# A relative-position bias that is shifted through DRAM, written and read back in four pieces

## What is computed

```python
delta = qi + BLOCK - kj
bucket = t5_causal_bucket(np.clip(delta, 0, steps) * dilation)
bias = jnp.transpose(rel_bias_table.astype(jnp.float32)[bucket], (2, 0, 1))
scores = jnp.einsum('brhnqd,brhnkd->brhnqk', qb, kw).astype(jnp.float32) * (dh ** -0.5)
scores = jnp.where(valid, scores + bias[None, None, :, None], NEG_INF)
```

```python
h = rmsnorm(x, g[0])
z = h @ w_in
za, zb, zc = jnp.split(z, [3 * A_WIDTH, 3 * A_WIDTH + 2 * B_WIDTH], axis=-1)
```

## Time and profile before

| | |
|---|---|
| median of 3 runs | 2355.29 us (2349.98 to 2355.97) |
| the profiled execution | 2355.84 us, span 2354.1 us |
| TensorE matmul busy | 2253.3 us, 96% of the span |
| VectorE, ScalarE, GpSimd busy | 1362.3, 1067.9, 62.9 us |
| mean granted clock of TensorE | 0.979 of full speed |
| moved by DMA | 375.59 MB, 160 GB/s over the span |

### The profile page before, as it was taken

How to read it: one execution, slowest core, us unless ns; L and a number is a source line. 1 busy time by engine, 2 the same in 40 slices (tenths; PEclk the granted TensorE clock), 3 DMA queues, 4 the chain that set the end, 5 groups by cost and what they waited for, 6 DMA issues and landing times.

```text
span 2354.1 us, 31707 instructions
## 1 busy us (share of the span) xinstructions
PE 2253.3 (96%) x12978; PEld 1959.9 (83%) x12978; DVE 1362.3 (58%) x1718; ACT 1067.9 (45%) x1376; POOL 62.9 (3%) x66
## 2 busy tenths in 40 slices
PE   8799999888989999999999999999999999999998
PEld 7788898787877888888888888888986889889776
DVE  5446666566556666767666444655445555544554
ACT  5343542424455544544555334545435443544443
POOL 0000101002000000000000000000000000000000
PEclk9899999899989999999999999999999999999999
DMA  7756440014634555555565555553550556445143
GB/s 279 189 191 202 163 158 1 1 32 154 203 118 134 190 185 188 186 187 187 186 206 191 190 192 196 185 195 120 181 178 19 180 178 222 159 152 174 59 129 140
DMA packets 237804, 375.59 MB, mean 160 GB/s; under 512 B 8535, under 2 KB 110072, under 8 KB 236920
## 3 DMA queue, kind: packets, MB, share of 16 engines
q1 hardware_dynamic: 229596, 362.83, 46.3%
q10 hardware_dynamic: 8092, 11.11, 1.9%
HBM read 369.45 MB, written 4.46 MB: 159 GB/s over the span
## 4 chain that ended last, share of the span: by engine, by line
PE 65%; issue 5%; DVE 4%; ACT 2%; POOL 0%; DVEq 0%; POOLq 0%; ACTq 0%
PE PS L482 16%; PE PS L441 12%; PE PS L443 12%; PE PS L442 12%; PE PS L485 8%; DVE w_lo L359 1%; PE PS L2062 1%; ACT w_hi L354 1%; PE PS L2152 1%; PE PS L2136 1%; PE PS L2046 1%; PE PS L2827 1%; DVE h_both L938 0%; PE PS L921 0%; ACT spare L2074 0%
## 5 line engine op out<-in xcount | busy, mean ns | idle before, releaser
L359 DVE TENSOR_TENSOR w_lo<-raw,w_hi 128x2048 fp32r<-128x2048 f32 (+2 forms) x340 | 766.8, 2256 | 765.2 <-ACT w_hi L354 765.0
L354 ACT ACTIVATE w_hi<-raw 128x2048 fp32r<-128x2048 f32 (+2 forms) x340 | 641.2, 1886 | 876.0 <-PE PS L443 494.4
L482 PE MATMUL PS<-h_both,w_hi 128*128 128x512 f32 x1968 | 541.6, 397 | 12.2 <-DVE w_lo L359 9.4
L441 PE MATMUL PS<-w_hi,h_both 128*128 128x512 f32 (+2 forms) x1344 | 514.9, 383 | 11.7 <-DVE h_both L943 4.5
L442 PE MATMUL PS<-w_lo,h_both 128*128 128x512 f32 (+2 forms) x1344 | 507.2, 377 | 0.0
L443 PE MATMUL PS<-w_hi,h_both 128*128 128x512 f32 (+2 forms) x1088 | 408.3, 375 | 0.0
L482 PEld LDWEIGHTS PS<-h_both,w_hi 128*128 128x128 f32 x1968 | 338.1, 190 | 59.4 <-ACT arena L609 9.6
L485 PEld LDWEIGHTS PS<-h_both,w_lo 128*128 128x128 f32 x1968 | 303.2, 189 | 42.2
L485 PE MATMUL PS<-h_both,w_lo 128*128 128x256 f32 x1968 | 314.0, 281 | 0.0
L441 PEld LDWEIGHTS PS<-w_hi,h_both 128*128 128x128 f32 x1344 | 254.3, 189 | 60.0 <-issue 6.0
L442 PEld LDWEIGHTS PS<-w_lo,h_both 128*128 128x128 f32 x1344 | 254.6, 189 | 45.4
(11 more groups left out here) (569 smaller groups left out, 2003.4 us busy)
## 6 DMA issues: line engine op xcount, KB each, us to landing
raw<-in_w_in SPq DMA_DIRECT2D x132, 1024.0 KB, 5.0
raw<-in_ffn_w_up SPq DMA_DIRECT2D x176, 512.0 KB, 4.3
raw<-in_w_out SPq DMA_DIRECT2D x48, 1024.0 KB, 5.1
raw<-in_ffn_w_down SPq DMA_DIRECT2D x44, 1024.0 KB, 5.0
raw<-in_mem_wkv SPq DMA_DIRECT2D x8, 1024.0 KB, 11.5
raw<-in_mem_wq SPq DMA_DIRECT2D x4, 1024.0 KB, 5.1
raw<-in_mem_wo SPq DMA_DIRECT2D x4, 1024.0 KB, 7.2
raw<-in_w_in SPq DMA_DIRECT2D x4, 768.0 KB, 4.6
```

The source lines that it names most:

```text
L354: act.activation(w_hi[:, slot % 2, :st.n], raw[:, slot, :st.n], ACT.Copy).then_inc(hi_made, 1)
L359: dve.tensor_tensor(w_lo[:, slot % 2, :st.n], raw[:, slot, :st.n], w_hi[:, slot % 2, :st.n].bitcast(F32), ALU.subtract).then_inc(lo_made, 1)
L441: pe.matmul(ps, l_hi, r_hi, start=start, stop=False, skip_group_check=skip)
L482: pe.matmul(sums, wh[:, k, cs], h_both[:, :, kk, :], start=kk == 0, stop=False, skip_group_check=True)
```

## The change

The write to DRAM is no longer one transfer of 12 heads but four of three heads each, and so is the read back. They are issued from a new function, `bias_scalar`, which is woven into the channel columns' stage: its steps follow ScalarE's splits of C0, C1, C2 and so on. A piece is written after C0, C2, C4 and C6; the wait for all four writes stands after C10; a piece is read back after C10, C11, C12 and C13. The semaphores are waited for at 64 in place of 16.

```diff
@@ -1842,7 +1842,7 @@
             if h < 2:
-                dve.wait_ge(rel_back, 16)
+                dve.wait_ge(rel_back, 64)
@@ -3174,6 +3174,22 @@
+        def bias_scalar(act):
+            for n in range(4):
+                hs = slice(3 * n, 3 * n + 3)
+                act.dma_start(shifted[hs], arena[hs, WROW:WROW + 384].unsqueeze(1).to_broadcast([3, P, 384]))\
+                   .then_inc(rel_out, 16)
+                yield
+                yield
+            yield
+            yield
+            act.wait_ge(rel_out, 64)
+            for n in range(4):
+                act.dma_start(rel_bias[:, 3 * n:3 * n + 3, :],
+                              bass.AP(shifted.tensor, 3 * n * 384 * P + P - 1, [[383, P], [384 * P, 3], [1, S]]))\
+                   .then_inc(rel_back, 16)
+                yield
@@ -3273,13 +3289,10 @@
             act.wait_ge(bias_job.dve, bias_job["copied"])
-            act.dma_start(shifted, arena[0:A_H, WROW:WROW + 384].unsqueeze(1).to_broadcast([A_H, P, 384])).then_inc(rel_out, 16)
             run(products_scalar(act, ST_BC, more=True, opening=opening_scalar(act, ST_BC, t_x, gain_of("g_mix"))))
-            act.wait_ge(rel_out, 16)
-            act.dma_start(rel_bias, bass.AP(shifted.tensor, P - 1, [[383, P], [384 * P, A_H], [1, S]])).then_inc(rel_back, 16)
-            run(products_scalar(act, ST_C, before=end_of(ST_BC), more=True))
+            weave(products_scalar(act, ST_C, before=end_of(ST_BC), more=True), bias_scalar(act))
             run(products_scalar(act, ST_CE, before=end_of(ST_C), more=True))
-            act.wait_ge(rel_back, 16)
+            act.wait_ge(rel_back, 64)
```

## The result

The changed kernel takes 2358.57 us (median of 16 runs, 2353.57 to 2363.92), the kernel before 2353.62 us beside it (16 runs). The ratio is 1.0024, with a 95% interval of 1.0017 to 1.0031: slower by 5 us. The forecast had the side and, by half a microsecond, the range; its size, +15 us, was three times too large.

The account below looks back on a forecast made before the run. TensorE was taken as the bound, busy 2253.3 of 2354.1 us. The profiled 2355.84 + 13 (C11 late, with lower clock) + 2 (loads) = 2371 us; range 2358 to 2422.

Parts of the forecast that it names:

- the old stall: TensorE's wait before C0, behind the bias write: 9.4 us idle plus 3.1 of lower clock, 12.5 us at most to win.
- step 6: Loads beside the write: up to 16 us, 2 taken; what is lost early is covered by the wait before C11.
- steps 2, 3, 5 and 6: First write's rows begin near 94; last row near 172; C11 9.9 us late plus 3.1 lower clock; loads add 2.
- the sum of 78 us: Length of the four writes on three shared engines, paced by partition groups: 23.4, 15.6, 15.6 and 23.4 us.
- the range of the mechanism itself: Three shared engines, 78 us of writing: 2365 to 2382, chance 0.54.
- 13 + 9 + 7: C11's late start and lower clock 13; up to 9 from loads slowing the write; up to 7 if C10's load is late.
- step 7: Three more reads and three more issues, 0.4 to 1.4 us each on ScalarE, were taken as hidden.
- The engine's own pace: Rival: each engine keeps 0.244 us per row, last row at 219, C11 60 us late: 2416; chance 0.19.
- Side by side: Rival: each write takes other engines, the fourth lands at 151, all 12.5 us won: 2343 to 2350; 0.16 with faster rows.
- the loads are the bound: Rival: loads held by writes starve TensorE, 2382 to 2410, chance 0.07; sign: waits at C4, C6, C8 longer than C11's.
- It cancels out: Rival: the last row of the writes comes near 160, time the same; chance 0.04.

Follow-up runs that it names:

- heads apart: Changed kernel with heads n, n+4, n+8 in each write, so the source partitions lie in three groups of four: 2339.12 us, ratio 0.9944.
- addresses apart: Changed kernel with neighbouring source partitions in each write, but written to and read from DRAM places n, n+4, n+8: 2358.22 us, ratio 1.0019.

## Why the prediction was right and wrong

**Right: what the old stall was worth.** 12.5 us were reckoned from 9.4 of idling and 3.1 of lower clock; without a write the kernel is 12.9 us faster.

**Right: three engines per piece, shared by all four, and groups of four partitions.** The 1548 packets and the 15 rows per us after the second issue show the first. The heads apart (2339) and the addresses apart (2358) show the second, on the source side, and the steps of 16, 33 and 49 rows per us with all four writes at once show it directly: three groups for twelve partitions. That engines are shared also shows with the heads apart: 60 packets moved from 96 to 99, ahead of the second issue, and 65 from 103 to 106, behind it. The Trainium skill's rules (DMA: Bandwidth & Descriptors, "Why a DMA increments its semaphore by 16 and not by 1"; SBUF — State Buffer, "Door 1: The DMA port swizzle") agree with these runs in the two things that bear on here: by the first three heads go on three engines, by the second four neighbouring partitions lie on one port. The lowest-numbered engines themselves were not seen.

**Right: the end of the write sets C11.** It was priced at 4.9 us from the wait's end to the first matmul; it was 171.0 - 166.2 = 4.8. The losses at C5 and C7 hardly count when the wait follows, as step 6 said of lost time there; that also makes the wait itself short, 8.5 us and not 27, since C10 is split at 156.3 and not at 144 to 146.

**Wrong: the size, in steps 2, 3, 5 and 6.** The step that failed most is the end of the last write, with the sum of 78 us behind it. The wait ended at 166.2, not at 173: 7 us. Some 2 are from the start, since I let the first write wait for C0's split to be finished, and it is issued as the split begins (88.37 for 89.8); its first rows move at 92.3 and not at 94. The other 5 are the length of the write, 73 us up to 165.7. I added 23.4 + 15.6 + 15.6 + 23.4 = 78 as if a piece could begin only when all three engines had left the one before, but an engine goes on to its next head as soon as it is through with one. The steps of the run with all four writes at once show it, and in the changed kernel itself 92 packets moved from 140 to 142, a rate that takes all three groups at once. Redone with engines that go on at once and share a group evenly, the same rates make 74 us by my estimate. That it comes so near is luck in part, as the sharing was not even. From 155 to 163 only 14 packets per us moved, in 5.8% of the 16 engines' time, nearly all that one engine has: one seems to have been left alone with the rest. Why it fell behind stays open.

The lower clock took 1.7 to 1.9 us of C11, not 3.1: the old stall's price was carried over to a wait of 3.5 us, where TensorE had idled 9.4. And the 2 us of step 6 did not come. So C11 was late by 3.0 (9.9 reckoned), and 3.0 + 1.9 = 4.9 us is what the medians show, 5.0. The gain of 12.5 and the loss of the new waits nearly cancel, so an error of 7 us in one end time was half of the forecast. That the kernel still came out slower is therefore luck in good part: with the wait three units later it came out level with the one before (2354.55, ratio 1.0002). The range holds the time by 0.6 us only because it was widened; the range of the mechanism itself, 2365 to 2382, misses it. By its own terms, 13 + 9 + 7 over 2355.84, its upper end would be 2385.

**Wrong: step 7, which hid the issues.** I priced the issues at 0.4 to 1.4 us. Two took 9.9 and 16.6 us, and they made two of TensorE's three waits, the ones at C5 and C7. They changed the time little only because the wait ahead of C11 covered them; with that wait moved, they cost 12 to 14 us by themselves, and with all four at once 36 us of ScalarE.

**The rivals.** The engine's own pace (2416) is out, since a row takes an engine 0.17 us with three engines in one group and 0.066 with each in its own (17.2% and 20.1% of the 16 engines' time for 64 and 195 packets in 4 us). "Side by side" is out too, for the pieces as they were cut; with the heads apart its time was nearly reached (2339 for 2343), but on the same three engines. The sign of "the loads are the bound" came near to being seen: TensorE's waits at C5 and C7, 4.1 and 4.0 us, are longer than the 3.5 at C11. But they come from the issues, not from loads. "It cancels out" wanted a last row near 160; it was written at 165.7, about halfway between that and 172, and the loss of 5 us is under the 7 us that the prediction gives to a measurement. So this rival, at 0.04, was as near as the forecast.

## What to carry to other kernels

A transfer from few partitions is as slow as the partitions are close: cut it so that a piece takes partitions of different groups of four, or get the small source to DRAM once and copy it there with a long outer dimension. Cutting a transfer into pieces along a short outer dimension cuts the engines, not the time, and the pieces queue up. And an issue is not free: with some 200 rows per DMA engine on its queue, an engine here stood in the next issue, and so did everything behind it, where no semaphore in the program tells of it. Where only the wait is in the way, look first for a later place for it: that alone won 10.7 us here, with the transfer left as it was.

## What was not expected of the hardware

- An issue on ScalarE took 0.7 to 1.4 us when at most 212 packets per DMA engine were outstanding as it began, its own 129 included. With 246, 265 and 317 it took 3.2, 9.9 and 16.6 us, and three in a row took 35.9.
- Three engines that read from one group of four partitions write 16 rows of 1536 bytes per us together, and 33 and 49 with two and three groups.
- A copy of 2.36 MB from DRAM to DRAM, in rows of 1536 bytes, all from the same 12 source rows, was over within the 14 us from 70 to 84, where the same rows from 12 partitions took 31 us.
- A load that needs 16 DMA engines was held by a write on only three of them nearly as long (19.2 us to landing, issued at 92.6) as by one on twelve (24.2 us).
